# Grouped heads' rotation by transfers through memory instead of permutation products, with three smaller edits

## The chip, the core and the metric

One core of one Trainium2 chip. The metric is the device time of one execution of the whole program in microseconds (us). The kernel before takes 945.94 us, the median of three runs (944.39 to 946.18). The engines are named as in the profile: PE is TensorE, PEld its weight loads, DVE is VectorE, ACT is ScalarE, POOL is GpSimd, and SP is the engine that issues most loads.

## The reference

Two layers of a diffusion trunk over 512 latent tokens and 256 context tokens, width 1024, all in float32. Each layer normalises and modulates its input, projects it to 2752 columns, feeds three branches (a gated linear attention, GLA; a latent attention, MLA; grouped-query attention, GQA), and adds their gated output projection. In the last layer the context isn't updated.

```python
for l in range(DEPTH):
    want_ctx = l < DEPTH - 1
    shift, scale, gate = split(silu(c) @ w_mod[l] + b_mod[l], 3)
    ...
    h = rms_norm(x, norm_w[l]) * (1.0 + scale) + shift
    u = split_cols(h @ w_in[l], IN_COLS)        # and uc from the context
    y_a, yc_a = gla_branch(...)                 # gates: log_sigmoid(a_f @ w_a_f + b_a_f), and a_b
    y_b, yc_b = mla_branch(...)                 # rms_norm(cq) @ w_uq, rms_norm(ckv) @ w_ukv
    y_c, yc_c = gqa_branch(...)                 # rms_norm per head, then rotation of q and k
    x = x + gate * (concat(y_a, y_b, y_c) @ w_out[l])
    if want_ctx:
        ctx = ctx + gate_c * (concat(yc_a, yc_b, yc_c) @ w_out[l])

def apply_rope_2d(x, cos, sin):                 # 64 features: two axes of two quarters of 16
    xr = x.reshape(x.shape[:-1] + (2, 2, q))
    x1, x2 = xr[..., 0, :], xr[..., 1, :]
    return stack([x1 * cos - x2 * sin, x2 * cos + x1 * sin], axis=-2)
```

## The kernel before

Everything lies transposed: features on the 128 partitions, tokens along the free dimension (T = 768, CTX the first 256, LAT the last 512). The input projection is cut into "units" of 128 columns: small (the two gate ranks of 16 and the shared rotary key), cq0, cq1, ckv0, ckv1 (the MLA's low ranks), gq0 to gq2 and gk (GQA's queries and keys), glaq, glak, tok (values, by token tile), and z0 to z7. Each unit's weights come by a 512 KB load of SP into one of four slots; ACT rounds them to a high part (L711) and DVE subtracts for the low part (L1152); PE takes three products for each of the eight blocks of 128 input features (L1644 to L1646).

All engines walk one list, `SEQ`, written out by hand, and each does its own part of every item. Engines run their own instructions in order and wait on semaphores; `at(stage, step)` is the count at which a step is done. PE's results go round a ring of six PSUM banks: `open_` waits until the group six places before was released.

The items around the change, in the order of `SEQ`:

- `ss0c`, `ss0l`, `ss1c`, `ss1l`: mean square of cq (0) and ckv (1) over 256 features, for context (c) and latent (l). ACT squares both blocks of 128 features into `sq` (L836), PE multiplies both by a matrix of ones and adds them in PSUM (L1717), ACT takes the inverse root (`rms`, L674 and L678), DVE scales (L1265). Layer 1 has no `ss0c`.
- `ga`: gate factors of both directions, four products of 32 rows (L1709); the weights `wa` hold 16 rows of one direction and 16 of zeros. ACT and DVE make log-sigmoids and cumulated sums of them (L817 to L822, L1222 to L1235), and `ga2` the exponentials (L826 to L829). `gq0` follows `ga`, `gq1` follows `ss1c`.
- `gss0` to `gss3`: mean squares of GQA's queries and keys (L1725), DVE scales (L1274).
- `kdT`, `rope0`, `tok5`, `rope1`, `z0`, `rope2`, `rope3`, `z1`: `rope<i>` rotates block i. PE multiplies the block by a permutation matrix, which exchanges features that differ by 16 (L1731); DVE takes the product times the sine (L1281), the block times the cosine (L1285), and adds (L1287). DVE's splits of z1's and z2's weights stand ahead of z0's gate, that of z3's weights behind rope3.

GpSimd, in the same stretch, fills `QK` with zeros (L555) after GLA's factors, waits for the transposes `kdT`, makes the block-diagonal factors of the first tile (`gla_in`, L525 and L532), and waits for z7. In the attention heads that follow, `mod_of_head` puts two blocks of the gate projection of the layer into heads 7 and 8; `mod_turn` turns its two rows (latent, context) into full tiles `gate` (L1618), and ACT copies them (L667).

## Time and profile before

| | us |
|---|---|
| median of three runs | 945.94 |
| lowest, highest | 944.39, 946.18 |
| profiled execution, its own time | 946.4 |
| its span, first to last instruction | 944.5 |
| PE busy | 900.5 (95%) |
| DVE busy | 530.3 (56%) |
| ACT busy | 416.2 (44%) |
| POOL busy | 161.1 (17%) |

The 16 DMA engines move 74.18 MB, a mean of 79 GB/s. An instruction's time in the groups holds its latency too, so that neighbours on PE overlap; what a group of matmuls adds to the run is its length in the chain. "x4" counts instructions; an f32 product is two instructions (two passes), a product of the rounded high and low parts is one.

### The profile page before, as it was taken

How to read it: one execution, taken by the hardware profiler on the slowest of the kernel's cores; microseconds unless marked ns; L12 is line 12 of the kernel's file. 1: busy time of each engine (PE TensorE's matmuls, PEld its weight loads, DVE VectorE, ACT ScalarE, POOL GpSimd, SP SyncE). 2: the span in 40 equal slices, each digit the busy share in tenths (PEclk: the TensorE clock that was granted, in tenths of full speed). 3: DMA queues.
4: the chain of work that ended last, by engine and by line, in shares of the span. 5: the costliest groups of instructions: out<-in, count | busy, mean ns of one | idle time of the engine just before them, and what ended most of it. 6: DMA issues, size and time to landing. Idle time of an engine off the chain costs nothing.

```text
span 944.5 us, 12656 instructions
## 1 busy us (share of the span) xinstructions
PE 900.5 (95%) x4511; PEld 657.7 (70%) x4511; DVE 530.3 (56%) x929; ACT 416.2 (44%) x773; POOL 161.1 (17%) x193
## 2 busy tenths in 40 slices
PE   3799999999999999999999999999999999899995
PEld 3488889888766666555588787889775656445584
DVE  4455534534467677867625745553546877556624
ACT  5435444321334444666732645443414435546712
POOL 1020000001262223002162000000017311002250
PEclk9899999999999999999999999999999999999998
DMA  9740130310202222222037112321402000222032
GB/s 344 281 126 24 45 90 23 91 49 21 90 1 90 90 90 90 90 97 81 1 120 196 45 41 50 91 66 30 124 7 88 1 1 1 90 90 90 0 112 90
DMA packets 67867, 74.18 MB, mean 79 GB/s; under 512 B 6148, under 2 KB 47456, under 8 KB 67680
## 3 DMA queue, kind: packets, MB, share of 16 engines
q1 hardware_dynamic: 61392, 60.24, 20.2%
q0 software_dynamic: 4016, 12.77, 3.8%
q8 instruction: 39, 0.64, 0.3%
q10 hardware_dynamic: 2400, 0.38, 0.2%
q14 instruction: 20, 0.16, 0.1%
HBM read 69.18 MB, written 4.19 MB: 78 GB/s over the span
## 4 chain that ended last, share of the span: by engine, by line
PE 87%; DVE 5%; ACT 3%; issue 2%; POOL 1%; ACTq 1%; DVEq 0%; POOLq 0%
PE pv L1868 12%; PE bank L1644 10%; PE bank L1646 10%; PE bank L1645 10%; PE bank L1956 4%; PE bank L1954 4%; PE bank L1955 4%; PE bank L1833 4%; PE bank L1799 2%; PE bank L1921 2%; PE bank L1915 2%; PE bank L1691 2%; PE bank L1690 2%; PE bank L1692 2%; PE bank L1595 2%
## 5 line engine op out<-in xcount | busy, mean ns | idle before, releaser
L1644 PE MATMUL bank<-hA_parts,W_parts 128*128 128x512 f32 (+1 forms) x480 | 175.3, 365 | 5.1 <-DVE h_low_parts L1144 5.1
L1645 PE MATMUL bank<-hA_parts,W_parts 128*128 128x512 f32 (+1 forms) x496 | 175.1, 353 | 0.0
L995 ACT ACTIVATE hA<-bank 128x512 f32<-128x512 f32 (+1 forms) x168 | 93.8, 564 | 130.6 <-PE bank L1917 78.2
L1443 DVE TENSOR_REDUCE mxp<-bank 128x1 f32<-128x384 f32 x192 | 95.9, 551 | 32.7 <-PE bank L1833 32.1
L1644 PEld LDWEIGHTS bank<-hA_parts,W_parts 128*128 128x128 f32 x480 | 92.8, 193 | 22.5 <-issue 10.8
L1646 PE MATMUL bank<-h_low_parts,W_parts 128*128 128x512 f32 (+1 forms) x300 | 106.7, 356 | 0.0
L1645 PEld LDWEIGHTS bank<-hA_parts,W_parts 128*128 128x128 f32 x496 | 95.9, 193 | 13.4 <-issue 1.9
L1868 PE MATMUL pv<-hA,vg 128*128 128x512 f32 (+1 forms) x168 | 81.6, 571 | 3.3 <-ACT hA L995 3.3
L1152 DVE TENSOR_TENSOR W_parts<-W,W_parts 128x1024 fp32r<-128x1024 f32 x43 | 52.5, 1222 | 37.6 <-ACT W_parts L711 37.5
L1868 PE MATMUL pv<-hA,h_low 128*128 128x512 f32 (+1 forms) x144 | 68.5, 556 | 0.0
L1646 PEld LDWEIGHTS bank<-h_low_parts,W_parts 128*128 128x128 f32 x300 | 58.0, 193 | 7.8
L711 ACT ACTIVATE W_parts<-W 128x1024 fp32r<-128x1024 f32 x43 | 45.3, 1056 | 40.5 <-DMA W<-in_w_in 40.1
L1955 PE MATMUL bank<-W_parts,hA_parts 128*128 128x512 f32 x160 | 62.3, 389 | 0.0
L802 ACT ACTIVATE tz<-bank 128x512 f32<-128x512 f32 (+1 forms) x24 | 12.7, 527 | 84.4 <-PE bank L1646 84.4
L692 ACT ACTIVATE tz<-XA 128x1024 f32<-128x1024 f32 x16 | 16.9, 1056 | 72.8 <-DVE XA L1538 72.8
L1200 DVE SCALAR_TENSOR_TENSOR YA<-tz,bank 128x512 f32<-128x512 f32 (+1 forms) x24 | 14.4, 598 | 57.8 <-ACT tz L802 57.8
L1833 PE MATMUL bank<-W_parts 96*128 96x384 f32 (+1 forms) x108 | 44.7, 496 | 0.8 <-DVE glaqk L1315 0.5
L1414 DVE SCALAR_TENSOR_TENSOR hA<-pv,hA 64x512 f32<-64x512 f32 (+1 forms) x36 | 21.6, 599 | 42.5 <-ACT hA L953 42.2
L1533 DVE TENSOR_TENSOR rt<-bank,cqkv 128x512 f32<-128x512 f32 x20 | 13.8, 688 | 54.5 <-DMA XA<-in_x 19.2
L1646 PE MATMUL bank<-rounded,W_parts 128*128 128x512 f32 (+1 forms) x120 | 42.0, 350 | 0.0
L1868 PEld LDWEIGHTS pv<-hA,vg 128*128 128x128 f32 x168 | 29.5, 190 | 16.3 <-ACT hA L995 6.8
L532 POOL TENSOR_TENSOR XA<-XA,con 128x512 f32<-128x512 f32 x10 | 12.2, 1222 | 148.8 <-DVE XA L1297 78.3
(291 smaller groups left out, 1898.2 us busy)
## 6 DMA issues: line engine op xcount, KB each, us to landing
W<-in_w_in SPq DMA_DIRECT2D x39, 512.0 KB, 4.0
W<-in_w_mod SPq DMA_DIRECT2D x8, 2048.0 KB, 8.0
W<-in_w_out SPq DMA_DIRECT2D x4, 2048.0 KB, 7.8
gqk<-in_w_mod SPq DMA_DIRECT2D x2, 1536.0 KB, 9.5
cqkv<-in_w_mod SPq DMA_DIRECT2D x2, 1536.0 KB, 13.9
XA<-in_x SPq DMA_DIRECT2D x4, 512.0 KB, 7.1
XA<-in_x POOLq DMA_DIRECT2D x4, 512.0 KB, 6.6
x_between_layers<-XA POOLq DMA_DIRECT2D x4, 512.0 KB, 2.9
```

The lines of the kernel that those rows point to most:

```text
L711: act.activation(unit_parts(l, u)[0], w_units[:, 0, slot], ACT.Copy).then_inc(*up("w_high", l, u))
L995: act.activation(prob[slot % 4][:, 0:nq], ps("sc", l, h, q0, kt)[:, 0:nq], ACT.Exp, scale=MLA_SCALE if h < MLA_H else GQA_SCALE)\
L1152: dve.tensor_tensor(rest, w_units[:, 0, slot], high.bitcast(F32), ALU.subtract)\
L1443: dve.tensor_reduce(mxp[:, t, half:half + 1], ps("mx", l, h, q0, t, half)[:, 0:384], AX, ALU.max).then_inc(*up("part_max", l, h, q0, t, half))
L1644: pe.matmul(p[:, 0:c[1]], high[:, k, :], h_hi[:, k, toks], start=(k == 0), stop=False)
L1645: pe.matmul(p[:, 0:c[1]], low[:, k, :], h_hi[:, k, toks], start=False, stop=False)
L1646: mm = pe.matmul(p[:, 0:c[1]], high[:, k, :], h_lo[k][:, toks], start=False, stop=(k == KD - 1))
L1833: close(pe.matmul(p[:, 0:n], q[:, t * P:t * P + P], k[:, n * half:n * half + n], start=True, stop=True), "mx", l, h, q0, t, half)
L1868: mm = pe.matmul(pv_banks[i % 2][:, 0:nq], v, prob[sl % 4][:, 0:nq], start=(kt == 0), stop=(kt == nkt - 1))
L1954: pe.matmul(p[:], hi, w_hi[n][k], start=(k == 0), stop=False)
L1955: pe.matmul(p[:], hi, w_lo[:, i % 2, k, :], start=False, stop=False)
L1956: mm = pe.matmul(p[:], lo, w_hi[n][k], start=False, stop=(k == KD - 1))
```

## The change

1. The four permutation products of each layer go. GpSimd writes the block twice into a memory tensor, one copy above the other in each group of 32 features, waits, and reads rows 16 to 47 of each group back: the features exchanged by 16. The targets are `rt[:, 1]` and the two halves of `sq`. DVE reads them there instead of PSUM.
2. GpSimd adds the two halves of `sq` before the product with ones; PE takes one product instead of two.
3. The second direction's gate weights move to rows 48 to 63 of `wa`, with zeros in 32 to 47; `small` holds its first 32 rows a second time in rows 32 to 63 (weights copied by GpSimd where they were set to zero). The four products now alternate between rows 0 to 31 and 32 to 63.
4. In the last layer the context's gate tile is neither multiplied nor copied.

```diff
+def gate_rows(layer):
+    return range(1 if layer == DEPTH - 1 else 2)
...
+        crossed = [rt[:, 1, :], sq[:, 0, :], sq[:, 1, :], rt[:, 1, :]]
+        turn_dram = [nc.dram_tensor(f"crossed_pairs{i}", [4, 64, NL_TOK], F32, kind="Internal").ap() for i in range(4)]
...
-                pool.dma_start(wa[RANK:2 * RANK, 1, :], a["gla_w_a_bwd"][l]).then_inc(*dma("wa_in", l))
+                pool.dma_start(wa[3 * RANK:4 * RANK, 1, :], a["gla_w_a_bwd"][l]).then_inc(*dma("wa_in", l))
...
-                pool.memset(w_units[:, 0, 0, :, 32:64], 0.0).then_inc(*up("swap_kr", l))
+                pool.tensor_copy(w_units[:, 0, 0, :, 32:64], w_units[:, 0, 0, :, 0:32]).then_inc(*up("swap_kr", l))
...
+                for item in seq_of(l):
+                    if item[:2] == "ss":
+                        j = int(item[2])
+                        for c in norm_chunk(item, "q" if j == 0 else "kv", l):
+                            pool.wait_ge(*at("lora_sq", l, j, c))
+                            pool.tensor_tensor(sq[:, 0, 0:c[1]], sq[:, 0, 0:c[1]], sq[:, 1, 0:c[1]], ALU.add)\
+                                .then_inc(*up("lora_sum", l, j, c))
+
                 pool.wait_ge(*at("con_in"))
                 pool.wait_ge(*at("gla_factors", l, 1))
                 pool.memset(QK[:, 0:1024], 0.0).then_inc(*up("bd_zero", l))
+                def cross(i):
+                    pool.wait_ge(*at("gqa_norm", l, i, LAT))
+                    pool.wait_ge(*at("kr_rope", l))
+                    pool.wait_ge(*(at("gqa_sin", l, 0) if i == 3 else at("filled", "gss", l, 3 if i else 0, LAT)))
+                    for s in range(2):
+                        pool.dma_start(turn_dram[i][:, 32 * s:32 * s + 32, :], gqk[:, i, 256:T]).then_inc(*dma("cross_out", l, i))
+                    pool.wait_ge(*at("cross_out", l, i))
+                    pool.dma_start(crossed[i], turn_dram[i][:, 16:48, :]).then_inc(*dma("crossed", l, i))
+
+                for i in range(4):
+                    cross(i)
                 pool.wait_ge(*at("filled", "kdT", l, 1, 1))
...
-                    for s in range(2):
+                    for s in gate_rows(l):
...
-                        dve.wait_ge(*at("filled", "rope", l, i))
+                        dve.wait_ge(*at("crossed", l, i))
                         dve.wait_ge(*(at("gqa_rope", l, i - 1) if i else at("kr_rope", l)))
-                        dve.tensor_tensor(rt[:, 0, :], ps("rope", l, i)[:], sing, ALU.mult)\
+                        dve.tensor_tensor(rt[:, 0, :], crossed[i], sing, ALU.mult)\
                             .then_inc(*up("gqa_sin", l, i))
-                        let_go(("rope", l, i), "gqa_sin", l, i)
...
-                        for d in range(2):
-                            for c in (CTX, LAT):
-                                p = open_("ga", l, d, c)
-                                close(pe.matmul(p[:, 0:c[1]], wa[:, d, :], small[0:32, c[0]:sum(c)], start=True,
-                                                stop=True), "ga", l, d, c)
+                        for c in (CTX, LAT):
+                            both = [open_("ga", l, d, c) for d in range(2)]
+                            for d, p in enumerate(both):
+                                r = slice(32 * d, 32 * d + 32)
+                                close(pe.matmul(p[:, 0:c[1]], wa[r, d, :], small[r, c[0]:sum(c)], start=True, stop=True),
+                                      "ga", l, d, c)
...
-                            pe.wait_ge(*at("lora_sq", l, j, c))
-                            for f in range(2):
-                                mm = pe.matmul(p[:, 0:c[1]], ones[:], sq[:, f, 0:c[1]], start=(f == 0), stop=(f == 1))
-                            close(mm, "ss", l, j, c)
+                            pe.wait_ge(*at("lora_sum", l, j, c))
+                            close(pe.matmul(p[:, 0:c[1]], ones[:], sq[:, 0, 0:c[1]], start=True, stop=True), "ss", l, j, c)
...
-                        i = int(item[4])
-                        p = open_("rope", l, i)
-                        pe.wait_ge(*at("gqa_norm", l, i, LAT))
-                        close(pe.matmul(p[:], perm, gqk[:, i, 256:T], start=True, stop=True), "rope", l, i)
+                        pass
```

TensorE in layer 0 from `ss0l` through `ga` to the start of `gq0`. Before:

```order
L1646 MATMUL bank0<-YA_parts,W_parts 128x512
L1717 MATMUL bank1<-sq,ones 128x512 x2
L1709 MATMUL bank2<-small,wa 128x256
L1709 MATMUL bank3<-small,wa 128x512
L1709 MATMUL bank4<-small,wa 128x256
L1709 MATMUL bank5<-small,wa 128x512
L1644 MATMUL bank0<-hA_parts,W_parts 128x256
```

And in the changed kernel, whose lines stand 25 or 26 further on:

```order
L1671 MATMUL bank0<-YA_parts,W_parts 128x512
L1742 MATMUL bank1<-sq,ones 128x512
L1735 MATMUL bank2<-small,wa 128x256
L1735 MATMUL bank3<-small,wa 128x256
L1735 MATMUL bank4<-small,wa 128x512
L1735 MATMUL bank5<-small,wa 128x512
L1669 MATMUL bank0<-hA_parts,W_parts 128x256
```

One of the two products with `ones` is gone, and the gate products go by chunk first and direction second.

GpSimd in layer 0, from the exchange of MLA's query weights (`wuq`) to the first factors of the GLA, with what each waits for. Before:

```order
L514 COPY wuq<-wuq 128x12x2x8 [waits wu_in]
L514 COPY wuq<-wuq 128x12x2x8
L555 MEMSET glaqk 128x1024 [waits gla_factors,con_in]
L525 ISA
L525 TENSOR_TENSOR XA<-XA,con 128x256 [waits filled]
```

And in the changed kernel, up to the second exchange; two more like it follow, and then the factors (L531):

```order
L564 TENSOR_TENSOR sq<-sq 128x256 [waits lora_sq]
L564 TENSOR_TENSOR sq<-sq 128x512 [waits lora_sq]
L564 TENSOR_TENSOR sq<-sq 128x256 [waits lora_sq]
L564 TENSOR_TENSOR sq<-sq 128x512 [waits lora_sq]
L569 MEMSET glaqk 128x1024 [waits gla_factors,con_in]
L576 DMA crossed_pairs<-gqk 4x32x512 [waits filled,kr_rope,gqa_norm]
L576 DMA crossed_pairs<-gqk 4x32x512
L578 DMA rt<-crossed_pairs 128x1x512 [waits cross_out]
L576 DMA crossed_pairs<-gqk 4x32x512 [waits filled,kr_rope,gqa_norm]
L576 DMA crossed_pairs<-gqk 4x32x512
L578 DMA sq<-crossed_pairs 128x1x512 [waits cross_out]
```

Four sums come ahead of the memset, and twelve transfers with their waits between it and the factors.

DVE in layer 1 from the second rotation to the split of z3's weights, in the changed kernel (L1178 is the split, L1226 z0's gate):

```order
L1307 TENSOR_TENSOR rt<-sq,con 128x512 [waits gqa_rope,crossed]
L1310 TENSOR_TENSOR gqk<-gqk,con 128x512 [waits gqa_norm]
L1312 TENSOR_TENSOR gqk<-gqk,rt 128x512 [waits gqa_cos]
L1178 TENSOR_TENSOR W_parts<-W,W_parts 128x8x128 [waits w_high] x2
L1226 SCALAR_TENSOR_TENSOR YA<-tz,bank 128x512 [waits ztanh]
L1307 TENSOR_TENSOR rt<-sq,con 128x512 [waits gqa_rope,crossed]
L1310 TENSOR_TENSOR gqk<-gqk,con 128x512 [waits gqa_norm]
L1312 TENSOR_TENSOR gqk<-gqk,rt 128x512 [waits gqa_cos]
L1307 TENSOR_TENSOR rt<-rt,con 128x512 [waits gqa_rope,crossed]
L1310 TENSOR_TENSOR gqk<-gqk,con 128x512 [waits gqa_norm]
L1312 TENSOR_TENSOR gqk<-gqk,rt 128x512 [waits gqa_cos]
L1178 TENSOR_TENSOR W_parts<-W,W_parts 128x8x128 [waits w_high]
```

The order is that of before; each rotation's first product waits for a transfer (`crossed`) where it waited for PE (`filled`).

## Rows read from the trace of the kernel before

**Rows 1.** Part 1 of the page, busy time of each engine.

```profile
PE 900.5 (95%) x4511; PEld 657.7 (70%) x4511; DVE 530.3 (56%) x929; ACT 416.2 (44%) x773; POOL 161.1 (17%) x193
```

**Rows 2.** Part 4 of the page, the chain that ended last, by engine.

```profile
PE 87%; DVE 5%; ACT 3%; issue 2%; POOL 1%; ACTq 1%; DVEq 0%; POOLq 0%
```

**Rows 3.** Chain in order of time, layer 0: start us, us, what.

```profile
83.80 1.72 PE bank L1717 x4
85.52 2.77 PE bank L1709 x8
...
98.33 0.86 PE bank L1717 x4
...
107.54 1.72 PE bank L1717 x4
```

**Rows 4.** Chain, alternating products L1763; wait from a GpSimd result to PE.

```profile
252.48 1.06 PE bank L1763 x8
...
729.10 0.24 issue
```

**Rows 5.** Stretch of layer 0: width, PE busy, granted clock, DMA share, GB/s.

```profile
88.00:92.00 4.00, 4.00 (x21) 0.61 0.00 0
```

**Rows 6.** Chain in order of time, layer 1, the same items.

```profile
580.60 2.77 PE bank L1709 x8
...
590.67 0.86 PE bank L1717 x4
...
597.01 1.72 PE bank L1717 x4
```

**Rows 7.** Timelines of ACT (both layers) and SP: start us, us, engine, line, operation.

```profile
101.98 0.85 ACT L829 ACTIVATE XA<-XA 128x768 f32<-128x768 f32 x1 [0.35 <-DVE XA L1242]
...
105.88 1.05 ACT L836 ACTIVATE sq<-cqkv 128x1024 f32<-128x1024 f32 x1
...
588.41 0.61 ACT L836 ACTIVATE sq<-cqkv 128x512 f32<-128x512 f32 x1
...
595.54 1.04 ACT L836 ACTIVATE sq<-cqkv 128x1024 f32<-128x1024 f32 x1
...
590.70 0.37 SPq L452 DMA_DIRECT2D W<-in_w_in  x1
```

**Rows 8.** GpSimd's groups (busy, mean ns); then timelines of GpSimd and DVE.

```profile
L525 POOL TENSOR_TENSOR XA<-XA,con 128x256 f32<-128x256 f32 x20 | 13.2, 680 | 37.5 <-PE bank L1739 36.9
...
L626 POOL DMA_DIRECT2D x_between_layers<-XA x4 | 2.2, 547 | 17.9 <-DVE XA L1538 17.9
...
216.02 1.95 POOL L532 TENSOR_TENSOR XA<-XA,con 128x512 f32<-128x512 f32 x1 [44.86 <-DVE XA L1297]
...
215.85 1.22 DVE L1152 TENSOR_TENSOR W_parts<-W,W_parts 128x1024 fp32r<-128x1024 f32 x1
```

**Rows 9.** Chain, layer 1: last sum of squares, rope1, rope2 with rope3.

```profile
646.03 0.86 PE bank L1725 x2
...
657.40 0.86 PE bank L1731 x2
...
663.74 1.72 PE bank L1731 x4
```

**Rows 10.** Timeline of DVE, layer 1: weight splits L1152, fourth rotation L1281.

```profile
662.66 1.23 DVE L1152 TENSOR_TENSOR W_parts<-W,W_parts 128x1024 fp32r<-128x1024 f32 x1 [2.35 <-ACT W_parts L711]
664.47 1.23 DVE L1152 TENSOR_TENSOR W_parts<-W,W_parts 128x1024 fp32r<-128x1024 f32 x1 [0.58 <-ACT W_parts L711]
...
669.10 0.69 DVE L1281 TENSOR_TENSOR rt<-bank,con 128x512 f32<-128x512 f32 x1
```

**Rows 11.** Part 6 / DMA view, GpSimd's queue: KB each, median us to landing.

```profile
x_between_layers<-XA POOLq DMA_DIRECT2D x4, 512.0 KB, 2.9
...
cqkv<-in_final_norm_w POOLq DMA_DIRECT2D x1, 512.0 KB, 7.9
```

**Rows 12.** Chain in order of time, gate rows in layer 1's heads.

```profile
838.76 1.72 PE bank L1618 x4
```

More of the change, by code:

```diff
@@ L284, in build @@
                         glav[:].rearrange("p t c -> p (t c)").rearrange("p (k n) -> p k n", k=3)[:, 0:2])]
-        wa = sb("wa", [32, 2, P])
+        wa = sb("wa", [64, 2, P])
         sq, sq_parts = twice("sq", [P, 2, 512])
@@ L555, in _ @@
                 pool.memset(QK[:, 0:1024], 0.0).then_inc(*up("bd_zero", l))
+                def cross(i):
[3 more added lines that the diff above has]
+                    for s in range(2):
+                        pool.dma_start(turn_dram[i][:, 32 * s:32 * s + 32, :], gqk[:, i, 256:T])                            .then_inc(*dma("cross_out", l, i))
+                    pool.wait_ge(*at("cross_out", l, i))
+                    pool.dma_start(crossed[i], turn_dram[i][:, 16:48, :]).then_inc(*dma("crossed", l, i))
+                for i in range(4):
+                    cross(i)
                 pool.wait_ge(*at("filled", "kdT", l, 1, 1))
@@ L1466, in gate_bias @@
                     dve.wait_ge(*at("brow_in", l))
-                    former = ("gate", l, 0, 1) if b == 5 else ("modT", l + 1, 3) if l + 1 < DEPTH else \
+                    former = ("gate", l, 0, gate_rows(l)[-1]) if b == 5 else ("modT", l + 1, 3) if l + 1 < DEPTH else \
                         ("gate", l - 1, 1, 1)
@@ L1614, in mod_turn @@
                 else:
-                    for s in range(2):
+                    for s in gate_rows(l):
                         q = open_("gate", l, b - 4, s)
```

## The prediction

> **What bounds the kernel now.** I read the page first: TensorE is busy 95% of the span [rows 1], and the chain that ended last is 87% TensorE [rows 2]. So a matmul taken away is worth its full time, unless what stands behind it isn't ready. I then read the chain in order of time around the changed lines, for the time that each group of matmuls really takes there; the timelines of ACT, DVE and SP, for when its neighbours are ready; and last GpSimd's rows, since that engine gets new work.
>
> The profiled execution took 946.4 us (span 944.5 and 1.9 around it), 0.5 over the median of the runs, 945.94. The sum is against 946.4. A measurement of this kernel tells about 0.2% (1.9 us) from no change.
>
> **Part 1: the rotation's products.** Each is one f32 product over 512 columns, two instructions, 0.86 us; in the chain rope1 of layer 1 takes 0.86 and rope2 with rope3 1.72 [rows 9]. Four in each of two layers: 8 x 0.86 = 6.88 us, all of it in the chain.
>
> What replaces them: for each, GpSimd issues two writes of 256 KB to memory, waits for both, and issues one read of 256 KB. An issue holds GpSimd 0.55 us [rows 8]. The nearest row for such a write is 2.9 us to landing for 512 KB, the slowest of this queue 7.9 us [rows 11]; I take 2.9 for each way, being nearest in kind. Then a next exchange can start 0.55 + 2.9 + 0.55 = 4.0 us after the last, and its data is there 0.55 + 2.9 + 2.9 + 0.55 = 6.9 us after its start. Exchanges 1 to 3 stand behind the last sum of squares of gk, whose product ends at 646.03 + 0.86 = 646.89 in layer 1 [rows 9]. They land at about 653.8, 657.8 and 661.8. DVE asks for the second rotation once rope1 was done (658.26, or 657.4 with rope0 gone), and for the fourth at 669.10, less the ropes about 666.5 [rows 10]. Margins 3.6 and 4.7 us: hidden. Exchange 0 waits for nothing of that stretch. In layer 0 z0 has two chunks, so the margins are no smaller. On GpSimd the first block-diagonal factors of the GLA (L525) are queued behind the waits; the block products that read them come after z7, 40 us later, and the factors' second half waits for DVE's states anyway.
>
> What is late next, where the stall-free product goes: z1's weights in layer 1. The SP queue asks for them when tok5 is done (657.40). Their low half is split by DVE at 662.66 to 663.89 [rows 10]. z0 takes 663.74 - 658.26 = 5.48 us, so with no ropes TensorE is at z1 at 657.40 + 5.48 = 662.88 and waits 1.0 us. Also exchange 3's read-back falls into the same transfers: two weight units come 664.47 - 662.66 = 1.8 us apart for 512 KB each, so 256 KB ahead of them costs up to 0.9; the nearest value between nothing and that is unknown, I take the middle, 0.5. In layer 0 z0 is 8.35 us long and this wait doesn't arise. Ropes: 3.44 + (3.44 - 1.5) = 5.4 us.
>
> **Part 2: one product for each sum of squares instead of two.** 256 columns cost 0.43, 512 cost 0.86 (chain: 0.86 for four instructions of 256, 1.72 for four of 512) [rows 3, 6]. Before it GpSimd must add the halves: 0.68 us for 256 columns and, by twice the elements, 1.36 for 512 [rows 8]. To this come about 0.1 us from ACT to GpSimd and 0.24 from GpSimd to TensorE [rows 4]: 1.0 and 1.7 us after ACT's square. A GpSimd product of 512 columns (L532) also took 1.95 us, while DVE was subtracting weights (L1152) [rows 8].
>
> The Trainium skill, "SBUF — State Buffer", section "SBUF: two separate sides", says that GpSimd and a DVE operation with two SBUF inputs take a shared port in turn. The 1.95 us fits that; by the page the 512 sums could each cost 0.6 more. It isn't in the sum.
>
> **Part 3: the gate products side by side.** Now they take 2.77 us in a layer [rows 3, 6]: twelve units of 0.215 us and 0.19 of gaps. Rows 32 to 63 of the array now hold the second direction. The trace has the same pattern in L1763, four f32 products of 256 columns that alternate between the halves of the rows: 1.06 us [rows 4], five units and not eight, so the second pass of one runs beside the first of the next. By that pattern eight units are left: 1.72 + 0.19 = 1.91, a saving of 0.86. Bounds: nothing (no overlap), and 1.4 (both directions wholly at once).
>
> **Part 4: the clock.** After both gate stretches, and nowhere else in those stages, the granted clock goes to 0.5 of 2.4 GHz, that is 1.2 GHz: the mean is 0.61 in 88 to 92 us [rows 5], and the chain shows the same slowing in layer 1. TensorE was busy before it, but with 32 of its rows for 2.77 us. The price by the chain: the 48 matmuls of gq0 in layer 0 take 98.33 - 88.29 = 10.04 us, the 48 of gq1 107.54 - 99.19 = 8.35, so 1.69; in layer 1 gq0 takes 590.67 - 583.37 = 7.30 and gq1 597.01 - 591.53 = 5.48, so 1.82 [rows 3, 6]. With a stretch of 1.91 us I think the clock stays (about 2 to 1).
> The Trainium skill, "TensorE: Matmul & The Clock Gate", Part 1, says the slow clock is the default and activity lifts it. The trace agrees, though here an engine that never stood still fell too. By that rule the shorter stretch is better, but the page can't say whether it suffices; that is the first rival below.
>
> **Part 5: what parts 2 to 4 are worth, since ACT is close behind.** Layer 0. Removed before ss1l: 0.43 (ss0c) + 0.86 (ss0l) + 0.86 (gates) + 1.69 (clock) + 0.43 (ss1c) = 4.27, so TensorE is at ss1l at 107.54 - 4.27 = 103.27. ACT's square ends at 106.93 [rows 7]. Its chain begins with ss0l (1.29 earlier) and goes through DVE's scans and the subtraction for which ACT already waits at 101.98 (0.35 us) [rows 7]; I make it about 2.9 earlier, 104.0. With 1.7 for the sum: 105.7. Wait 2.4. With the product itself (0.86) removed the stage gains 5.13 - 2.43 = 2.7 us and not 5.1.
> Layer 1. Removed 0.86 + 0.86 + 1.82 = 3.54 before ss1c: TensorE is there at 590.67 - 3.54 = 587.13. ACT's square ended at 589.02 [rows 7]; it follows ss0l, so 588.16, and with 1.0 for the sum 589.16: wait 2.0. Then ss1l: TensorE at 589.16 + 0.43 + 5.48 = 595.07. ACT's square there waits for weights that SP asks for at the end of gq0 (issue 590.70, square's end 596.58, 5.88 later) [rows 7], now 593.0, with the sum 594.7: no wait. Gain 3.54 + 0.43 + 0.86 - 2.0 = 2.8 us.
>
> **Part 6: layer 1's context gate.** Two products of 512 columns fewer (four of them in pairs of 1.72 [rows 12]): 1.72 us. ACT and DVE lose copies there too. If DVE's maxima bounded those heads it would be nothing; the chain is TensorE's through them. The copy in place of a memset on 32 columns is some tenths on an idle GpSimd: nothing.
>
> Sum: 2.7 + 2.8 + 5.4 + 1.7 = 12.6 us; 946.4 - 12.6 = 933.8 us.
>
> **Rivals.**
> A, the clock still falls. For: it did both times. Then layer 0 removes 3.44, waits 106.05 - 104.96 = 1.1, gains 2.4; layer 1 waits 0.2 and then 1.5 (square's end 594.86, sum 596.56, TensorE 595.07), gains 3.01 - 1.7 = 1.3. Sum 2.4 + 1.3 + 5.4 + 1.7 = 10.8: 935.6 us. Most of the clock's gain is hidden by the waits, so this rival is near.
> B, the sums and transfers are dearer: sums at 1.95 (0.6 twice) on top of A, and exchange 3 delays weights by the full 0.9 and some rotation by another us: 937 to 940 us.
> C, nothing waits: ACT's chain moves fully forward. Then 5.13 + 4.83 + 6.88 + 1.72 = 18.6: 927.8 us. Against: ACT and DVE stand back to back in that stage. Half of it gives 930 to 931.
> D, slower: the exchanges hold DVE up in front of the weight splits. One mechanism: rope1 stands before z1's split and rope3 before z3's. With L for each way's landing an exchange starts every L + 1.1 and lands 2L + 0.55 after its start. At L = 9 us, in layer 1: exchange 1 at 665.5, split 3.2 later at 668.7, z1 late by 5.8; exchange 3 at 685.7, split 689.0 against 679.6, 9.4 more. Layer 0 by the same working 2.9 + 3.6. Together 21.7 less 12.6: 9 us slower, 955. It turns at about L = 8; at 7.9 (the slowest row) the gain is just gone. For: one row of 7.9. Against: that row is behind four others in its queue.
> E, no change: something in the heads takes it all back. Nothing speaks for it; 945.
>
> **How the numbers follow.** Forecast 933.8: 0.45, own range 931.5 to 936. A 0.21, B 0.14, C or half of it 0.12, D 0.04, E 0.04. The range 930 to 938.5 leaves out D, E, half of B and part of C: about 0.2. Faster by over 0.2% is everything but D and E: 0.92; within 0.03; slower 0.05 (D and a little of B's tail).
>
> **What would show it.** No rope line on TensorE, 1.9 us for the gate stretch, a granted clock of 1.0 behind it. TensorE idle before ss1l of layer 0 (about 2.4 us) and ss1c of layer 1 (2.0), ended by GpSimd; idle before z1 of layer 1 (1 to 2), ended by DVE's split. Exchanges landing 7 us after their first issue, and no DVE wait for a rotation. Wrong if the exchanges take over 10 us each, if the gate stretch still takes 2.7, or if TensorE waits nowhere.

## The result: 957.61 us, 1.3% slower

| kernel | median us (runs) | lowest to highest | ratio to before, 95% |
|---|---|---|---|
| before | 946.06 (4) | 944.39 to 946.26 | 1 |
| changed | 957.61 (4) | 957.37 to 960.02 | 1.0132 [1.0119, 1.0145] |

The forecast was 933.8 us, and a gain with a chance of 0.92. The change costs 11.5 us instead. The profiled execution of the changed kernel was its slowest (960.02 us); its span is 958.0 us against 944.5, so the traces have 13.5 us to explain. The runs of the kernel before that stand beside the experiments lie, one of 2545.6 us aside, in two groups, 943.8 to 944.8 us at a mean granted clock of 0.993 and 945.1 to 946.5 at 0.989 to 0.991, so a difference of a microsecond or two between kernels of different sets is not safe.

The page of the profile of the changed kernel first, parts 1 and 4, answering to [rows 1, 2]:

```profile
PE 892.6 (93%) x4477; PEld 654.3 (68%) x4477; DVE 529.9 (55%) x929; ACT 414.9 (43%) x771; POOL 187.3 (20%) x224
...
PE 82%; DVE 6%; ACT 5%; issue 4%; POOL 2%; ACTq 1%; DVEq 0%; POOLq 0%
```

TensorE has less to do (892.6 us, not 900.5) and yet less of the chain is its own: 82%, not 87%. The work went, and waits came. To place them I take two lines of the program whose instructions stand at the two ends of the stretch with the rotations: the transposes of `kd` (they follow the last sum of squares of gk) and the first query product of the heads. Rows of one line in a window: engine, operation, count, shortest/median/longest ns, first and last start. The kernel before, layer 0 and then layer 1:

```profile
L1739 PE MATMUL bank<-con,XA x12: 270/272/273, 168.4 to 169.6; 128*128 128x128 f32 x12
...
L1799 PE MATMUL bank<-cqkv,wuq x48: 377/486/592, 247.2 to 353.2; 128*128 128x256 f32 x24, 128*128 128x512 f32 x24
...
L1739 PE MATMUL bank<-con,XA x12: 272/273/273, 650.9 to 652.1; 128*128 128x128 f32 x12
...
L1799 PE MATMUL bank<-cqkv,wuq x24: 590/592/593, 706.6 to 793.3; 128*128 128x512 f32 x24
```

The changed kernel, the same:

```profile
L1760 PE MATMUL bank<-con,XA x12: 272/272/273, 168.0 to 169.2; 128*128 128x128 f32 x12
...
L1820 PE MATMUL bank<-cqkv,wuq x48: 377/486/593, 249.0 to 355.0; 128*128 128x256 f32 x24, 128*128 128x512 f32 x24
...
L1760 PE MATMUL bank<-con,XA x12: 272/272/273, 652.1 to 653.3; 128*128 128x128 f32 x12
...
L1820 PE MATMUL bank<-cqkv,wuq x24: 590/592/593, 722.1 to 808.7; 128*128 128x512 f32 x24
```

From the transposes to the first query product takes 78.8 us before and 81.0 after in layer 0, 55.7 and 70.0 in layer 1. So the exchange stretch lost 2.2 + 14.3 = 16.5 us. Up to the transposes layer 0 gained 0.4, and between 247.2 and 650.9 (249.0 and 652.1 now) 0.6. After the last of these lines it gained 237.9 - 235.9 = 2.0, of which the gate rows are 1.7. 16.5 - 0.4 - 0.6 - 2.0 = 13.5.

**The exchange.** The transfers by line, count, KB and median us from issue to landing, then the queue of GpSimd (packets, MB, share), both of the changed kernel:

```profile
q0 software_dynamic: 10544, 19.10, 6.5%
...
crossed_pairs<-gqk POOLq DMA_DIRECT2D x16, 256.0 KB, 7.8
rt<-crossed_pairs POOLq DMA_DIRECT2D x4, 256.0 KB, 6.1
sq<-crossed_pairs POOLq DMA_DIRECT2D x4, 256.0 KB, 7.0
```

Each way takes 6 to 8 us, not the 2.9 of [rows 11]. The 7.8 is a median over pairs: the first write of a pair lands 3.2 to 5.4 us after its issue in six of the eight, the second, which the exchange waits for, 7.7 to 9.0 us in all eight. GpSimd's timeline in layer 1 shows how they queue (start, us, engine, line, operation, idle before and what ended it):

```profile
648.82 1.37 POOL L576 DMA_DIRECT2D crossed_pairs<-gqk  x2 [3.40 <-PE bank L1749]
657.63 0.71 POOL L578 DMA_DIRECT2D sq<-crossed_pairs  x1 [7.44 <-DMA crossed_pairs<-gqk]
658.33 1.37 POOL L576 DMA_DIRECT2D crossed_pairs<-gqk  x2
668.39 0.70 POOL L578 DMA_DIRECT2D sq<-crossed_pairs  x1 [8.69 <-DMA crossed_pairs<-gqk]
669.34 1.38 POOL L576 DMA_DIRECT2D crossed_pairs<-gqk  x2 [0.25 <-issue]
678.36 0.70 POOL L578 DMA_DIRECT2D rt<-crossed_pairs  x1 [7.64 <-DMA crossed_pairs<-gqk]
```

An exchange starts every 9.5 to 11 us, and its features are there 16 to 17 us after its start. DVE stands for them, and behind the rotation in its queue stand the weight splits L1178 (DVE of the changed kernel, layer 1, answering to [rows 10]):

```profile
666.07 0.69 DVE L1307 TENSOR_TENSOR rt<-sq,con 128x512 f32<-128x512 f32 x1 [7.37 <-DMA sq<-crossed_pairs]
...
668.01 2.35 DVE L1178 TENSOR_TENSOR W_parts<-W,W_parts 128x1024 fp32r<-128x1024 f32 x2
...
685.47 0.69 DVE L1307 TENSOR_TENSOR rt<-rt,con 128x512 f32<-128x512 f32 x1 [9.30 <-DMA rt<-crossed_pairs]
...
687.41 1.22 DVE L1178 TENSOR_TENSOR W_parts<-W,W_parts 128x1024 fp32r<-128x1024 f32 x1
```

The chain there, where [rows 9] had the rotations' products, and the stretches behind its idle pieces (width, PE busy, then the other engines, granted clock, DMA share, GB/s):

```profile
663.24 6.09 issue
...
682.79 5.94 issue
```

```profile
665.00:670.00 5.00, 0.67 (x2) 0.60 (x3) 3.89 (x5) 3.29 (x3) 1.36 (x2) 0.75 1.01 297
670.00:675.00 5.00, 5.00 (x15) 3.94 (x14) 1.90 (x4) 1.65 (x3) 0.72 (x2) 0.57 0.60 124
...
690.00:695.00 5.00, 5.00 (x13) 3.92 (x13) 2.10 (x3) 0.00 (x0) 0.00 (x0) 0.52 0.01 3
```

TensorE stands before z1 and before z3, 12.0 us in all, and after each stop it works at 0.5 of 2.4 GHz, that is 1.2 GHz, for five or six microseconds more: a matmul of 512 columns takes 0.43 us in the chain and not 0.23. With 10 and 12 such matmuls that is another 4.4 us. 12.0 + 4.4 - 3.44 (four products gone) = 13.0 of the 14.3; the first matmul after each stop adds 0.3 (0.77 us in the chain, 0.47 after e6's stop below). In layer 0, where z0 and z1 are longer, the stops are 3.48 (at 181.94) and 0.23 us.

**The sums.** What stood at [rows 7] and [rows 3]: TensorE waits for GpSimd before the product of the key and value part in both layers (PE of the changed kernel), and the clock falls behind both stops:

```profile
104.92 2.05 PE L1742 MATMUL bank<-sq,ones 128*128 128x512 f32 x2 [2.73 <-POOL sq L564]
...
591.34 0.67 PE L1742 MATMUL bank<-sq,ones 128*128 128x256 f32 x2 [2.65 <-POOL sq L564]
```

```profile
105.00:110.00 5.00, 5.00 (x18) 3.97 (x19) 1.62 (x3) 2.57 (x4) 0.00 (x0) 0.50 0.10 29
110.00:115.00 5.00, 5.00 (x26) 4.40 (x26) 1.35 (x2) 0.00 (x0) 0.00 (x0) 0.89 0.00 0
...
590.00:595.00 5.00, 3.66 (x11) 2.99 (x12) 4.97 (x6) 1.84 (x3) 1.12 (x1) 0.74 0.37 101
```

The waits are near those that the prediction gave (2.4 and 2.0); the half clock behind them is not in it. Nor is the time that GpSimd and DVE lose beside each other (GpSimd, then DVE, layer 1 of the changed kernel):

```profile
590.07 1.12 POOL L564 TENSOR_TENSOR sq<-sq 128x256 f32<-128x256 f32 x1 [14.62 <-ACT sq L862]
```

```profile
590.65 2.16 DVE L1261 TENSOR_TENSOR_SCAN cumA<-keep,XA 128x768 f32<-128x768 bf16 x1
```

The sum of 256 columns takes 1.12 us, nearly as much as that of 512 at 596.55 (1.29, with DVE idle beside it), and not the 0.68 of [rows 8]. It started 0.54 us before DVE's subtraction of two operands in the core's memory (L1254) ended. DVE's scan behind that takes 2.16 us, and 1.76 in every kernel whose GpSimd has no key and value sum; the scan is in the chain of the gates that ACT's next square follows.

**The gates.** PE, from the start of the eight products to the next unit's first, and the stretch behind them, answering to [rows 3, 5]:

```profile
83.31 1.56 PE L1735 MATMUL bank<-small,wa 32*128 32x256 f32 x8
84.79 0.39 PE L1669 MATMUL bank<-hA_parts,W_parts 128*128 128x256 f32 x1
```

```profile
85.00:90.00 5.00, 5.00 (x34) 4.62 (x34) 4.63 (x6) 4.87 (x8) 0.00 (x0) 1.00 0.00 0
```

They take 84.79 - 83.31 = 1.48 us instead of 2.77, and the clock stays at 2.4 GHz. The gate rows of layer 1 were two pairs in [rows 12] and are two single products now, the predicted 1.7 us:

```profile
854.18 0.86 PE bank L1643 x2
...
867.23 0.86 PE bank L1643 x2
```

### The profile page after: what moved, and what is told of

Read it like the earlier page. It is cut to its first block, busy times and chain, and to the rows that moved or that the text cites. A ratio compares the mean times of both kernels' runs of the same rounds, so it can differ in the third digit from the quotient of the medians.

```text
span 958.0 us, 12617 instructions
## 1 busy us (share of the span) xinstructions
PE 892.6 (93%) x4477; PEld 654.3 (68%) x4477; DVE 529.9 (55%) x929; ACT 414.9 (43%) x771; POOL 187.3 (20%) x224
## 2 busy tenths in 40 slices
DMA packets 74394, 80.50 MB, mean 84 GB/s; under 512 B 11140, under 2 KB 52448, under 8 KB 74208
## 4 chain that ended last, share of the span: by engine, by line
PE 82%; DVE 6%; ACT 5%; issue 4%; POOL 2%; ACTq 1%; DVEq 0%; POOLq 0%
PE pv L1889 12%; PE bank L1669 10%; PE bank L1670 9%; PE bank L1671 9%; PE bank L1977 4%; PE bank L1976 4%; PE bank L1975 4%; PE bank L1854 4%; PE bank L1820 2%; PE bank L1942 2%; PE bank L1936 2%; PE bank L1716 2%; PE bank L1717 2%; PE bank L1715 2%; PE bank L1620 2%
## 5 line engine op out<-in xcount | busy, mean ns | idle before, releaser
L1669 PE MATMUL bank<-hA_parts,W_parts 128*128 128x512 f32 (+1 forms) x480 | 177.4, 370 | 20.8 <-issue 15.7
L1670 PE MATMUL bank<-hA_parts,W_parts 128*128 128x512 f32 (+1 forms) x496 | 177.8, 358 | 0.0
L1669 PEld LDWEIGHTS bank<-hA_parts,W_parts 128*128 128x128 f32 x480 | 94.7, 197 | 39.4 <-issue 27.4
L1670 PEld LDWEIGHTS bank<-hA_parts,W_parts 128*128 128x128 f32 x496 | 97.8, 197 | 12.9 <-issue 1.2
L1178 DVE TENSOR_TENSOR W_parts<-W,W_parts 128x1024 fp32r<-128x1024 f32 x43 | 52.2, 1220 | 29.0 <-ACT W_parts L737 29.0
L1558 DVE TENSOR_TENSOR rt<-bank,cqkv 128x512 f32<-128x512 f32 x20 | 13.8, 688 | 54.4 <-DMA XA<-in_x 19.2
L1226 DVE SCALAR_TENSOR_TENSOR YA<-tz,bank 128x512 f32<-128x512 f32 (+1 forms) x24 | 14.1, 596 | 45.3 <-ACT tz L828 45.3
L1854 PEld LDWEIGHTS bank<-W_parts 96*128 96x128 f32 x108 | 20.1, 188 | 23.3 <-issue 21.4
```

The lines of the kernel that those rows point to most:

```text
L1178: dve.tensor_tensor(rest, w_units[:, 0, slot], high.bitcast(F32), ALU.subtract)\
L1669: pe.matmul(p[:, 0:c[1]], high[:, k, :], h_hi[:, k, toks], start=(k == 0), stop=False)
L1670: pe.matmul(p[:, 0:c[1]], low[:, k, :], h_hi[:, k, toks], start=False, stop=False)
L1854: close(pe.matmul(p[:, 0:n], q[:, t * P:t * P + P], k[:, n * half:n * half + n], start=True, stop=True), "mx", l, h, q0, t, half)
```

## Experiments

Three sets, each on one chip with its own runs of the kernel before. The stretches are from the transposes of `kd` to the first query product, read as above.

| kernel | median us | ratio to before, 95% | stretch L0 | stretch L1 |
|---|---|---|---|---|
| before (the two traces above) | | 1 | 78.8 | 55.7 |
| changed | 957.61 | 1.0132 [1.0119, 1.0145] | 81.0 | 70.0 |
| e1 no exchange | 943.81 | 0.9983 [0.9973, 0.9993] | 78.7 | 55.7 |
| e2 exchange alone | 959.45 | 1.0144 [1.0130, 1.0159] | 80.9 | 69.0 |
| e3 gates and gate rows alone | 941.23 | 0.9950 [0.9937, 0.9963] | 78.7 | 55.8 |
| e5 e3, copies by SyncE | 951.33 | 1.0057 [1.0045, 1.0069] | 81.1 | 61.8 |
| e4 changed, transfers in four | 951.32 | 1.0067 [1.0055, 1.0080] | 75.8 | 64.8 |
| e6 e3, copies by GpSimd | 938.70 | 0.9935 [0.9921, 0.9949] | 75.3 | 54.1 |
| e7 e3, sums of the query part | 940.79 | 0.9953 [0.9941, 0.9966] | 78.7 | 55.8 |
| e9 changed, copies by GpSimd | 940.01 | 0.9943 [0.9929, 0.9956] | 75.3 | 53.9 |
| e8 e9, sums of the query part | 935.69 | 0.9897 [0.9879, 0.9914] | 75.3 | 54.2 |
| e10 changed, rows outermost | 944.76 | 0.9994 [0.9986, 1.0003] | 75.3 | 61.2 |

Set one (before 946.3): e1, e2, e3, e5. Set two (944.53): e4, e6, e7. Set three (945.81): e9, e8, e10.

### e1: the change without the exchange

```diff
-                for i in range(4):
-                    cross(i)
...
-                        dve.tensor_tensor(rt[:, 0, :], crossed[i], sing, ALU.mult)\
+                        dve.tensor_tensor(rt[:, 0, :], ps("rope", l, i)[:], sing, ALU.mult)\
...
+                        close(pe.matmul(p[:], perm, gqk[:, i, 256:T], start=True, stop=True), "rope", l, i)
```

> The changed kernel with its exchange undone: the features of the rotation come again from products with the permutation; the sums on GpSimd, the paired gate products and the missing gate rows stay. Theory T (the loss of 11.5 us is the exchange's, whose transfers land late, and the rest of the change is worth little): 943 to 946 us, of which 1.7 us are the gate rows at the end. Rival R (the prediction's own parts 5 and 6 held, so sums, gates and rows together give 7.2 us and the exchange costs 19): 938 to 940 us. Rival S (the sums' idle time on TensorE costs more than the exchange): 950 us or more.

943.81 us, 13.8 less than the changed kernel's median on the other chip; by ratios the exchange costs 1.0132 - 0.9983 = 1.5%, 14 us. The rest of the change together is worth 0.17%, about 1.6 us, no more than the gate rows alone. Theory T holds, R and S fall.

### e2: the exchange alone

Sums, gates and gate rows go back to the code before; the diff is the remainder of the change.

> The kernel before with the exchange through memory alone; sums, gate products and gate rows as before. Theory T: layer 0 of the changed kernel loses about 2.2 us in the heads' normalisation and layer 1 about 13 us, with nothing given by the rest, so 957 to 961 us. Rival S (sums, not the exchange): 941 to 946 us, since 6.9 us of products are gone.

959.45 us: the exchange alone is, by the ratio, 13.6 us slower than before, with nearly the changed kernel's stretches (80.9 and 69.0 us). It needs no help from the sums to lose the time, and theory T holds.

### e3: the gates and gate rows alone

```diff
-                            pe.wait_ge(*at("lora_sum", l, j, c))
-                            close(pe.matmul(p[:, 0:c[1]], ones[:], sq[:, 0, 0:c[1]], start=True, stop=True), "ss", l, j, c)
+                            pe.wait_ge(*at("lora_sq", l, j, c))
+                            for f in range(2):
+                                mm = pe.matmul(p[:, 0:c[1]], ones[:], sq[:, f, 0:c[1]], start=(f == 0), stop=(f == 1))
+                            close(mm, "ss", l, j, c)
```

(on top of e1; GpSimd's sums go too)

> The kernel before with the paired gate products and without the gate rows of the last layer; exchange and sums as before. Theory T' (the sums on GpSimd give TensorE 3.4 us less work per launch but idle time of 2.8 us per layer after which it works at half clock, so they are worth nothing or less): 940 to 943 us, 1.7 for the rows and 1.3 or more per layer for the gates and the clock behind them, and at least as fast as the kernel that has the sums as well. Rival (sums worth the 1.3 us per layer that their products take less): 1 to 3 us slower than that kernel.

941.23 us, by the ratio 4.7 less than before, and 2.6 less than e1 in the same set. Theory T' holds, the rival falls. The sums therefore cost 2.6 us although TensorE has 4.7 us less of products with them (0.43 + 0.86 + 0.43 + 0.86 in layer 0 and 0.86 + 0.43 + 0.86 in layer 1; the expectation had this too low at 3.4). PE and the stretch behind in e3:

```profile
105.07 1.96 PE L1724 MATMUL bank<-sq,ones 128*128 128x512 f32 x4 [0.45 <-ACT sq L842]
```

```profile
105.00:110.00 5.00, 4.93 (x30) 3.96 (x31) 2.72 (x6) 2.57 (x4) 0.00 (x0) 1.00 0.40 105
```

TensorE stands 0.45 us for ACT instead of 2.7 for GpSimd, and the clock stays at 1.00, against 0.66 in e1:

```profile
105.00:110.00 5.00, 4.18 (x16) 3.24 (x17) 1.46 (x3) 2.33 (x4) 0.67 (x1) 0.66 0.28 84
```

### e5: straight copies, issued by SyncE

```diff
+            def cross(l, i):
...
+                for b in range(8):
+                    o = 16 * (b ^ 1)
+                    sp.dma_start(crossed[i][16 * b:16 * b + 16], gqk[o:o + 16, i, 256:T])\
+                        .then_inc(*dma(f"crossed{i}", l))
...
+                    if u == UNIT_OF["z1"]:
+                        for i in range(4):
+                            cross(l, i)
                     unit_dma(l, u)
```

> Gate products paired and gate rows gone as in the run beside it, sums as before, and the exchange as straight copies inside the core's own memory, eight of 16 partitions for each group of heads, issued by SyncE ahead of the load of the first gated-attention output weights. Theory T (only the length of the round trip through memory, 7.8 us out and 6 to 7 back, made the exchange late; one leg of about 3 us is hidden): 4 to 6 us faster than the kernel beside it that keeps the products, 935 to 938 us. Rival U (VectorE is late with the groups' rotations whatever the transfer takes, since buffers are shared and the copies come after the wait for them): no faster than that kernel, or slower. Rival V (a transfer of single-core memory to itself also takes 6 us or more): 945 us or more.

951.33 us, 10 more than e3: T is wrong by its number. U and V have the number but not the cause: the copies land 2.0 us after their issue, and DVE waits for none. SyncE's queue shows what happened (layer 0):

```profile
142.46 5.01 SPq L468 DMA_DIRECT2D rt<-gqk  x8
162.12 9.99 SPq L468 DMA_DIRECT2D sq<-gqk  x16
172.22 4.95 SPq L468 DMA_DIRECT2D rt<-gqk  x8
177.22 33.93 SPq L458 DMA_DIRECT2D W<-in_w_in  x7
```

The output weights from z1 on (L458) are behind 32 issues of 0.62 us each and the waits of the exchange, so TensorE stood 4.03 us at 180.00 for weights, and 7.45 us at 660.75 in layer 1. Not the transfer, but what it stands in front of, set the time.

### e4: each transfer in four

```diff
-                        pool.dma_start(turn_dram[i][:, 32 * s:32 * s + 32, :], gqk[:, i, 256:T])
+                        for g in range(4):
+                            pool.dma_start(turn_dram[i][g, 32 * s:32 * s + 32, :], gqk[32 * g:32 * g + 32, i, 256:T])\
...
-                    pool.dma_start(crossed[i], turn_dram[i][:, 16:48, :])
+                    for g in range(4):
+                        pool.dma_start(crossed[i][32 * g:32 * g + 32], turn_dram[i][g, 16:48, :])\
```

> The changed kernel, each transfer of the exchange cut by 32-partition groups: eight writes of 32 rows and four reads of 32 partitions for each group of heads instead of two writes and one read over all four groups. Theory F (the trace shows 64 packets of 4 KB of a write on only four of the 16 DMA engines, since the outermost dimension of the pattern is 4): with 32 rows outermost all engines take part and a transfer of the pieces lands in 2.5 to 4 us after its issue, so a round trip takes 8 to 11 us instead of 15 to 17 and the kernel comes to 946 to 951 us. Rival G (the landing time is that of a small write to memory with its issues by GpSimd, not of the share of engines): 7 us or more a leg, and 957 us or more, as GpSimd has twelve issues of about 0.7 us per group instead of three.

951.32 us, just past F's range. The pieces land fast (DMA view of e4):

```profile
crossed_pairs<-gqk POOLq DMA_DIRECT2D x64, 64.0 KB, 2.0
rt<-crossed_pairs POOLq DMA_DIRECT2D x16, 64.0 KB, 2.1
sq<-crossed_pairs POOLq DMA_DIRECT2D x16, 64.0 KB, 2.1
```

but GpSimd spends 12 issues of 0.49 us, 5.9 us a group, and the last exchange is still late: layer 1 has a stop of 8.53 us at 670.68. F holds for the landing and G falls; the number of issues is a second cost, and a third is given under e10.

### e6: the straight copies, issued by GpSimd

The eight copies of e5, word for word, but `pool.dma_start` where the changed kernel has its exchange; SyncE's list is as before.

> The same kernel as the last one with straight copies (eight of 16 partitions per group of heads, no round trip; gates paired, gate rows gone, sums as before), but issued by GpSimd, so that SyncE's loads of the output weights are not held behind the exchange. In the run with SyncE the first of these loads was issued at 177.2 us, behind 28 issues of 0.62 us and a wait of 14.6 us, and TensorE stood 4.03 us. Theory T (the exchange costs only what it delays; on a free queue it is hidden): faster than the kernel with products by 3 to 6 us of its 6.9 us of products, 935 to 939 us. Rival U (shared buffers and the clock after TensorE's new waits for the output weights eat the gain whatever the queue): 940 to 943 us, the same as the kernel with products.

938.70 us, 0.65% below before and within T's range. The copies are hidden once their queue holds nothing else up (GpSimd in layer 0: 32 issues, done by 173.7 us, and DVE waits for none). The stretches are 75.3 and 54.1 us: 3.4 and 1.7 us (against e3) gained, so U's mechanism is not there. T's gain of 3 to 6 us over the kernel with products is not there in the medians either: by the ratios e6 is only 1.4 us below e3, and their intervals overlap; the rest is lost elsewhere, as the last section shows. Two pairs measured later, alike but for the exchange, give 3.8 us (e1 and e9) and 5.3 us (e7 and e8) by the ratios. In the chain of layer 1 one stop is left, before z1:

```profile
654.64 1.56 issue
```

### e7: sums of the query part alone, with products for the rotation

```diff
-                        for c in norm_chunk(item, "q" if j == 0 else "kv", l):
+                        for c in norm_chunk(item, "q", l) if j == 0 else ():
                             pool.wait_ge(*at("lora_sq", l, j, c))
...
-                            pe.wait_ge(*at("lora_sum", l, j, c))
-                            close(pe.matmul(p[:, 0:c[1]], ones[:], sq[:, 0, 0:c[1]], start=True, stop=True), "ss", l, j, c)
+                            pe.wait_ge(*at("lora_sum", l, j, c) if j == 0 else at("lora_sq", l, j, c))
+                            for f in range(1 if j == 0 else 2):
+                                mm = pe.matmul(p[:, 0:c[1]], ones[:], sq[:, f, 0:c[1]], start=(f == 0), stop=(f == j))
+                            close(mm, "ss", l, j, c)
```

> Products for the rotation, gates paired, gate rows gone, and the squares' sum on GpSimd only for the query part, not for the key and value part, whose sum left TensorE idle for 2.8 us in each layer, with half the clock behind it. Theory I (that idle stretch and its clock are what made the kernel with all sums 3 us slower than the one with none): 939 to 942 us, as fast as the kernel without sums or up to 1 us faster. Rival J (the sums hold up VectorE or GpSimd wherever they stand, or the query part's waits cost as much): 943 us or more, as the kernel with all sums.

940.79 us; the ratio 0.9953 is that of e3 (0.9950) and below that of e1 (0.9983). Theory I holds: the query part's sums do no harm, the key and value part's do. The traces show more: e7 is ahead of e3 by 1.2 us up to the transposes of layer 0 and by 0.8 from the first query product there to the transposes of layer 1, and loses 1.7 behind the first query product of layer 1, where the clock dips (last section). The stretch that was at 0.66 in e1 is, in e7:

```profile
105.00:110.00 5.00, 5.00 (x33) 4.28 (x32) 2.76 (x4) 2.58 (x4) 0.00 (x0) 1.00 0.33 93
```

### e9: the change whole, with the straight copies

The edit of e6 on the changed kernel, sums kept.

> The changed kernel whole (sums, gates, gate rows and exchange), with one thing put otherwise: the exchanged features come by eight straight copies of 16 partitions per group of heads, issued by GpSimd, instead of the round trip through memory. Theory T (the round trip's two legs, of about 8 and 6.5 us, are the loss; the sums cost some 3 us of their own): 940 to 943 us. Rival (the sums and the exchange hurt one another, since both are GpSimd's and both are waited for by VectorE): 946 us or more.

940.01 us. One edit, the way of the exchanged features, turns 1.32% slower into 0.57% faster: about 18 us. The theory holds: the sums and the exchange don't hurt one another.

### e8: what was found to help, together

The edit of e7 on e9.

> All parts that were found to give something: straight copies issued by GpSimd for the rotation, gates paired, gate rows gone, and the squares summed on GpSimd for the query part only. Theory: sums of the query part are worth 0 to 1 us beside the kernel with straight copies and no sums, so 937 to 939 us, 6 to 7 us faster than before. Rival (the query part's sums delay something that only the rotation's products covered): 940 us or more.

935.69 us, the fastest kernel of this study, 1.0% below before and 4.3 below e9 in the same set (the key and value part's sums again). Better than its theory by 1.3 us. The stop before z1 in layer 1 stays (1.63 us at 652.94).

### e10: the same round trip, rows outermost

```diff
-        turn_dram = [nc.dram_tensor(f"crossed_pairs{i}", [4, 64, NL_TOK], F32, kind="Internal").ap() for i in range(4)]
+        turn_dram = [nc.dram_tensor(f"crossed_pairs{i}", [2, 144, NL_TOK], F32, kind="Internal").ap() for i in range(4)]
...
-                        pool.dma_start(turn_dram[i][:, 32 * s:32 * s + 32, :], gqk[:, i, 256:T])
+                        pool.dma_start(turn_dram[i][s, 16 * s:16 * s + 128, :], gqk[:, i, 256:T])\
...
-                    pool.dma_start(crossed[i], turn_dram[i][:, 16:48, :])
+                    for b in range(8):
+                        o = 16 * (b ^ 1)
+                        pool.dma_start(crossed[i][16 * b:16 * b + 16], turn_dram[i][0, o:o + 16, :])\
```

> The changed kernel whole, with the round trip laid out otherwise: each of the two writes of 256 KB per group goes to rows that follow one another, so that 128 rows and not four groups are outermost, and the way back is eight reads of 16 rows. Theory F (the four engines, by the outermost dimension, are what a write's 7.8 us consists of): a write of the same 256 KB lands in 2.5 to 4 us, the round trip takes 9 to 11 us, and the kernel comes to 946 to 952 us. Rival G (such a write to memory takes 7 to 8 us anyway): 957 us or more.

944.76 us, below F's range and 13 us below the changed kernel; G falls. The DMA view of e10, for the same two writes of 256 KB:

```profile
crossed_pairs<-gqk POOLq DMA_DIRECT2D x16, 256.0 KB, 2.7
rt<-crossed_pairs POOLq DMA_DIRECT2D x32, 32.0 KB, 1.9
sq<-crossed_pairs POOLq DMA_DIRECT2D x32, 32.0 KB, 3.2
```

The writes take 2.7 us instead of 7.8, for the same bytes, number of writes, engine and queue. Two stretches in which hardly anything but such a pair of writes was under way show more, first of the changed kernel, then of e10 (the last two numbers are the DMA engines' share and GB/s):

```profile
649.00:657.00 8.00, 8.00 (x52) 7.97 (x51) 3.13 (x6) 2.52 (x6) 1.19 (x2) 1.00 0.34 73
```

```profile
642.40:644.00 1.60, 1.60 (x11) 1.60 (x11) 0.47 (x1) 0.00 (x0) 0.00 (x0) 1.00 0.87 323
```

0.34 of 16 engines are 5.4 packets at a time, 0.87 are 13.9. The fourth exchange is still late. Its way back has eight issues (3.9 us), and it meets the loads of the output weights: the second writes of six pairs land after 2.7 to 3.2 us, but that of layer 1's fourth, issued at 656.76 while weights come, after 6.1, and the reads before them after 4.4 to 5.5 us instead of 1.9. So DVE waits 4.95 and 6.66 us for it, and TensorE stops 4.21 us at 668.22 in layer 1, with the clock at 0.68 behind. Layer 0 loses nothing (75.3 us).

## Why the prediction was wrong

The forecast gain was 12.6 us and the traces lost 13.5, a difference of 26.1 us. Part 1 was to gain 5.4 and lost 16.5, which makes 21.9 of it; parts 2 to 5 were to gain 5.5 and gained 1.0, 4.5 more; behind layer 1's first query product the gain was 0.3 larger than part 6 had it.

**Part 1, the ropes: the step that failed.** "I take 2.9 for each way, being nearest in kind." The products were sized rightly: with copies that land early the stretch gains 3.4 us in layer 0, as stated, and 1.7 to 1.8 in layer 1, for 3.44 - 1.5 forecast; the stop before z1 is 1.56 us. What was mis-sized is the landing: 7.8 us out and 6 to 7 back. The 2.9 us row is a write of 512 KB from all 128 partitions in one run of rows; the exchange's patterns have the four groups of 32 rows outermost. e10 shows that this is the difference. The packet records of one such transfer hold 64 packets of 4 KB, and 192 of 8 bytes, which e10's writes lack; the page of the profile bears the count out. Its packets under 512 B went from 6148 to 11140 for 24 transfers, 208 each; in e10 it is 7428 for 80 transfers, 16 each.

The Trainium skill, "DMA: Bandwidth & Descriptors", in the section "Why a DMA increments its semaphore by 16 and not by 1", says that a transfer is spread over the largest number of engines, up to 16, that divides the slowest dimension of both its patterns. By that rule [4, 32, 512] goes over four. The trace agrees as far as it goes: the records don't name the engine, but the mean share is 0.22 of 16 engines, 3.5 packets at a time, while a read of the exchange runs alone (162.0 to 165.5 us), and 13.9 for the two writes of e10. The prediction should have weighed it. Why the second write of a pair takes so much longer than the first wasn't tried.

**Rival D was the case, with 0.04.** Its place, order and mechanism are what the trace shows: rope1 before z1's split, rope3 before z3's. It put the turn at a landing of about 8 us, and at 7.8 and 6 to 7 the kernel already loses 11.5. Its case of L = 9 is what came: features of the second and fourth rotation at 665.5 and 685.7 us, measured 666.07 and 685.47, and 21.7 us for both layers, measured 5.4 + 16.5 = 21.9. Shorter legs did what it gives for 9, since three terms were short. An exchange holds GpSimd for 2 x 0.69 + 0.70 us of issues, not 3 x 0.55. The second exchange begins at 648.82 us and not at 646.89. And the half clock behind each stop, some 4.4 us in layer 1, was priced for the gates but not for this rival's own stops. That the total agrees to 0.2 is luck: the stops are shorter than its own (12.0 for 15.2 in layer 1), and the clock makes up for it. The bounds from the rows were 2.9 and 7.9; between ends so far apart, an end at which the sign turns deserved more than 1 in 25.

**Part 2 and part 5, the sums.** The waits were nearly right (forecast 2.4 and 2.0, measured 2.7 and 2.7), and so was the time of a sum of 512 columns before ss1l (1.36 us), but by luck: it was had as twice the 0.68 of 256 columns, and those take 1.12 to 1.25. In the changed kernel a sum that starts beside a DVE operation on two operands in the core's memory is longer by about what is left of that operation: of 512 columns 1.29 us with DVE idle and 1.80 with 0.65 left, of 256 columns 1.12 with 0.54 left and 1.25 with 0.65. That is the delay which part 2 named and left out of its sum, and it is 0.44 of the 0.65 us by which layer 1's wait came out longer (2.65 for 2.0). Missing altogether were the scan of DVE, 0.4 us longer beside the sum, and the clock: TensorE idle for 2.7 us came back at 1.2 GHz for some six microseconds in layer 0 and four in layer 1. So the stage up to the transposes gained 0.4 us in layer 0 and not 2.7, and layer 1 with what stands between gained 0.6 and not 2.8. By the ratios the sums as built cost 3.1 us beside products (e3 and e1) and 0.8 beside straight copies (e6 and e9, not clear of noise); the key and value part alone costs 2.8 (e7 and e1) and 4.3 (e8 and e9).

**Part 3** was within its bounds: 1.48 us, between the forecast 1.91 and the bound 2.77 - 1.4. **Part 4** was right: no fall behind the gates in either layer of the ten kernels that pair them. But the fall isn't certain without the pairing: e2 has the old products, and its clock stays at 1.00 behind them in layer 0 (88 to 92 us, where before has 0.61) and falls in layer 1. With it goes that e2 reaches the transposes of layer 0 at 167.2 us and before, with the same code up to there, at 168.4; the gain of 0.4 above is no surer than that. Without the sums these parts and the gate rows bring e3's 4.7 us. **Part 6** was right to a tenth.

Rivals A and E are out: the clock fell, but behind the new stops and not behind the gates. B had dearer sums and transfers, which is the kind of thing that came, but with prices of at most a microsecond each. C, nothing waits, is nearest to e8, which still is 8 us from its 927.8.

## What to carry to other kernels

Before pricing a transfer by another one's row, compare their patterns: the outermost dimension on both sides, and not only bytes and direction. A transfer of small pieces that is put on a queue costs its issues (0.5 to 0.7 us each here) to whatever stands behind it there, so choose the queue with nothing urgent behind. And when a product on TensorE is traded for work elsewhere, price the stop twice: the idle time and the slow clock after it.

## What was not expected of the hardware

- The same 256 KB to memory land in 7.8 us with four rows of the pattern outermost and in 2.7 with 128 (medians over eight pairs of writes each).
- A copy of 16 partitions within the core's own memory (32 KB) takes 1.8 to 2.0 us to land, from either queue, and a group of eight is issued in 3.8 (GpSimd) to 5.0 us (SyncE).
- The clock behind a stop of TensorE, over the twelve traces and leaving out the stop at 28 us that all have: half clock followed all ten stops of 3.4 to 8.6 us, seven of the ten of 2.6 to 2.8 (not in layer 1 of e1, e9 and e10), six of the thirteen of 2.0 to 2.1, and none of 1.0 to 1.7.
- A GpSimd sum of 256 columns took 1.12 us beside a DVE operation and one of 512 took 1.29 with DVE idle, and DVE's scan beside the sum took 2.16 us instead of 1.76.
- A dip in layer 1's heads comes and goes between kernels that are the same there. All twelve traces have a stop of 2.0 us in the same place (811.0 us before). In e4 to e9 half clock follows it, and from the first query product to the gate rows they take 133.3 to 133.6 us; in the other six it doesn't, and they take 131.9 to 132.1. In e6 the clock is 0.83 where it is 1.00 in e3:

```profile
800.00:810.00 10.00, 8.01 (x24) 5.07 (x23) 5.73 (x10) 6.09 (x11) 0.00 (x0) 0.83 0.01 2
```

```profile
800.00:810.00 10.00, 7.74 (x27) 4.31 (x26) 5.53 (x10) 5.26 (x9) 0.73 (x1) 1.00 0.01 2
```

That is most of why e6 lies only 2.7 us of span below e3 (936.6 and 939.3), with 5.1 us gained in the two stretches. Why half clock follows that stop in some kernels and not in others wasn't tried and stays open.
